# Dilated attention: transposing the probabilities by a product with a diagonal of reciprocal sums

## What is computed

```python
for g, (win, dil) in enumerate(((128, 1), (512, 4), (2048, 16))):
    l = einsum(q * scale, k at q_idx - j * dil) + bias
    p, lse = masked_softmax(l, ok)            # exp(l - m) / sum
    o[g], lses[g] = einsum(p, v), lse
alpha = softmax(stack(lses), axis=0)
o = sum(alpha[..., None] * stack(o))
```

## Time and profile before

| | us |
|---|---|
| median of 3 runs | 1618.79 (1618.61 to 1619.01) |
| the profiled execution | 1611.5 |
| its span | 1609.8 |
| mean granted clock of PE | 0.986 |
| PE busy | 94% of the span |
| DVE, ACT busy | 22%, 22% |

### The profile page before, as it was taken

How to read it: one execution, slowest core, us unless ns; L and a number is a source line. 1 busy time by engine, 2 the same in 40 slices (tenths; PEclk the granted TensorE clock), 3 DMA queues, 4 the chain that set the end, 5 groups by cost and what they waited for, 6 DMA issues and landing times.

```text
span 1609.8 us, 24769 instructions
## 1 busy us (share of the span) xinstructions
PE 1520.3 (94%) x9164; PEld 1186.2 (74%) x9164; DVE 361.7 (22%) x1112; ACT 347.9 (22%) x932; POOL 158.8 (10%) x268
## 2 busy tenths in 40 slices
PE   8998999989899999999988989999889999999996
PEld 5656577767677987777975657777657789777786
DVE  1332234433011211100113242444220122110002
ACT  1132422234111211000123252222331112110003
POOL 2132420000000100000202424000000010000000
PEclk9999999999899999999999999999999999999999
DMA  9686568444355375565847454853716635655543
GB/s 265 155 194 156 150 216 279 151 159 144 126 187 182 106 257 186 187 232 187 244 127 178 121 153 123 291 180 122 239 56 205 215 105 173 243 192 183 196 162 132
DMA packets 212271, 288.06 MB, mean 179 GB/s; under 512 B 13781, under 2 KB 201383, under 8 KB 210888
## 3 DMA queue, kind: packets, MB, share of 16 engines
q1 hardware_dynamic: 194262, 189.01, 38.7%
q10 hardware_dynamic: 7858, 72.49, 12.0%
q0 software_dynamic: 10048, 25.19, 5.8%
HBM read 276.74 MB, written 72.49 MB: 217 GB/s over the span
## 4 chain that ended last, share of the span: by engine, by line
PE 82%; DMA 7%; issue 3%; DVE 2%; ACT 1%; POOLq 1%; SPq 1%; POOL 0%; ACTq 0%; DVEq 0%
PE psum L1469 77%; PE psum L1473 5%; DMA pages<-in_cache_nsa_kv 3%; DMA kv_ring<-in_cache_dil_w 1%; DMA w_ring<-in_w_in 1%; POOLq L702 1%; DMA w_ring<-in_w_ff 1%; ACT regrouped L838 1%; DMA arena<-in_x_sample 0%; DVE pt L1348 0%; SPq L506 0%; SPq L511 0%; DMA kv_ring<-in_cache_nsa_win 0%; SPq L471 0%; ACT xT L1052 0%
## 5 line engine op out<-in xcount | busy, mean ns | idle before, releaser
L1469 PE MATMUL psum<-arena,w_ring 128*128 128x144 f32 (+4 forms) x3584 | 684.1, 353 | 10.1 <-DVE arena L1404 4.8
L1469 PEld LDWEIGHTS psum<-arena,w_ring 128*128 128x128 f32 x3584 | 578.3, 190 | 110.5 <-DVE arena L1404 5.2
L1469 PE MATMUL psum<-xT,w_ring 128*128 128x288 f32 (+1 forms) x1472 | 358.4, 400 | 4.6 <-DMA w_ring<-in_w_in 4.6
L1469 PEld LDWEIGHTS psum<-xT,w_ring 128*128 128x128 f32 x1472 | 269.5, 191 | 80.1 <-issue 9.7
L779 POOL TENSOR_TENSOR arena<-arena 128x144 f32<-128x144 f32 x24 | 11.7, 487 | 653.6 <-DVE arena L1409 653.6
L1444 DVE TENSOR_TENSOR arena<-arena 128x288 f32 x64 | 29.3, 458 | 199.9 <-ACT arena L1062 199.9
L1062 ACT ACTIVATE arena<-psum 128x288 f32<-128x288 f32 x64 | 26.3, 410 | 197.3 <-PE psum L1469 197.3
L1195 DVE COPY arena<-psum 128x512 f32<-128x512 f32 x66 | 45.6, 692 | 78.4 <-PE psum L1473 78.2
L1469 PE MATMUL psum<-arena 64*128 64x128 f32 (+6 forms) x276 | 59.3, 342 | 0.0
L1447 DVE SCALAR_TENSOR_TENSOR arena<-arena,psum 128x288 f32<-128x288 f32 (+1 forms) x20 | 7.0, 390 | 223.0 <-PE psum L1469 223.0
L1473 PE MATMUL psum<-ident,regrouped 128*128 128x128 f32 (+1 forms) x300 | 48.3, 282 | 8.6 <-ACT regrouped L838 7.6
(11 more groups left out here) (206 smaller groups left out, 1214.7 us busy)
## 6 DMA issues: line engine op xcount, KB each, us to landing
w_ring<-in_w_ff SPq DMA_DIRECT2D x64, 1024.0 KB, 5.3
w_ring<-in_w_in SPq DMA_DIRECT2D x44, 1024.0 KB, 7.8
out<-in_cache_dil_w ACTq DMA_DIRECT2D x8, 1984.0 KB
pages<-in_cache_nsa_kv POOLq DMA_DIRECT2D x64, 192.0 KB, 4.5
pages<-in_cache_nsa_kv SPq DMA_DIRECT2D x64, 192.0 KB, 4.5
kv_ring<-in_cache_dil_w SPq DMA_DIRECT2D x20, 512.0 KB, 5.0
w_ring<-in_w_o SPq DMA_DIRECT2D x8, 1024.0 KB, 6.2
out<-in_cache_nsa_win ACTq DMA_DIRECT2D x8, 992.0 KB
```

The source lines that it names most:

```text
L1469: return T.matmul(out, w, x, start=start, stop=stop, **kw)
```

## The change

In dilated steps and in the sample rows' tail, DVE no longer multiplies the exponentials by the reciprocal sums. It multiplies the 128x128 identity by them, which gives a diagonal matrix `diag` (two halves, kept in `kcT`). PE then takes each block of exponentials as weights and the diagonal as the moving operand of an ordinary product, which gives the transposed and scaled block at once. The sparse steps (n < 16) stay as they were.

```diff
+        diag = kcT[:, 0:256].rearrange("p (x n) -> p x n", x=2)
@@ p_scale, n >= 16
-                        v = logit[:, L:L + 768].rearrange("p (g n) -> p g n", g=3)[:, :, 0:nk]
-                        V.tensor_scalar(v, v, S[:, 6:7], None, ALU.mult).then_inc(prob.sem, 1)
+                        V.tensor_scalar(diag[:, par], ident[:, :], S[:, 6:7], None, ALU.mult).then_inc(prob.sem, 1)
@@ the sample rows' tail, DVE
-                V.tensor_scalar(dlogit, dlogit, S[:, 14:15], None, ALU.mult).then_inc(dd_prob.sem, 1)
+                V.tensor_scalar(diag[:, 0], ident[:, :], S[:, 14:15], None, ALU.mult).then_inc(dd_prob.sem, 1)
@@ p_transpose, PE
-                            last = tr(bank(6 + k // 4, 128 * (k % 4), 128), logit[:, L + 256 * i + 128 * m:L + 256 * i + 128 * m + 128])
+                            out, p = bank(6 + k // 4, 128 * (k % 4), 128), logit[:, L + 256 * i + 128 * m:L + 256 * i + 128 * m + 128]
+                            last = tr(out, p) if n < 16 else mm(out, p, diag[:, par])
@@ the sample rows' tail, PE
-                    tr(bank(k // 4, 128 * (k % 4), 128), dlogit[:, 128 * k:128 * k + 128])
+                    mm(bank(k // 4, 128 * (k % 4), 128), dlogit[:, 128 * k:128 * k + 128], diag[:, 0])
                 for k in range(7, 10):
-                    last = tr(bank(k // 4, 128 * (k % 4), 128, 0, ND), dlogit[:, 896 + 32 * (k - 7):928 + 32 * (k - 7)])
+                    last = mm(bank(k // 4, 128 * (k % 4), 128, 0, ND), dlogit[:, 896 + 32 * (k - 7):928 + 32 * (k - 7)], diag[:, 0])
```

## The result

The changed kernel takes 1.0044 of the kernel before, 95% interval 1.0032 to 1.0056: slower by 7.1 us (5.2 to 9.1) of some 1619. Forecast were 8.7 us more, in a range of 3.6 to 12.8.

A forecast was written before the change was run, and what follows sets the result against it. PE was taken to bound the kernel. Per layer 4 x 0.70 + 2 x 0.38 + 1.13 - 0.34 = 4.35 us, two layers 8.70, added to 1618.8: 1627.5 us, range 1622.4 to 1631.6.

The forecast's parts named there:

- What bounds the stretch: Steps 16 to 23 and tail: PE's executed work sets the time; DVE's scaling is hidden in seven of eight steps.
- the 0.34 us: Step 23: DVE's shorter scaling cuts PE's wait from 1.87 to 1.53 us, once per layer.
- The count of passes: The 36 + 10 transpositions per layer on PE become products, one pass each becoming two.
- The rivals of one pass and of four passes: New products on PE: one pass, 1618.1 us (chance 0.04), or four per call, 1646.3 us (chance 0.01).
- The price: Added PE time per block, 0.108 us a pass: even step +0.38, odd step +0.70, tail +1.13 us.
- What is swallowed: Steps 16 and 18: existing DMA waits absorb the added 0.38 us each, so both are priced at nothing.
- The clock: PE around steps 16 and 23 and tail: low-clock losses stay in the sum; one fall more costs some 1.4 us.
- a rival that gives back 4.3 us: Around steps 16 and 23: denser PE work keeps the clock from falling, giving 1623.2 us; chance 0.16.
- DVE's rival: Steps 16 to 23 and tail: each transposition follows DVE's scaling, so 2.6 us per layer return, 1613.6 us; chance 0.03.

The follow-up runs named there:

- DVE's half alone: Kernel before, with DVE scaling the identity and PE still transposing, so the dilated branch is left without its division; against the kernel before: 1.0001 (0.9984 to 1.0018).
- PE's half alone: Kernel before, with the 36 + 10 transpositions per layer made products with the identity, DVE scaling as before; against the kernel before: 1.0056, +9 us.
- the doubled products: Changed kernel with each new product issued twice into the same place: 1.0192 of the kernel before, 24 us above the changed kernel.

## Why the prediction was right, and where its size was off

**What bounds the stretch: right.** DVE's half alone changed nothing that could be measured (1.0001), PE's half alone cost what the whole did, within the intervals (1.0056 and 1.0044). Only step 23 waited for DVE's scaling, and its wait shrank by the 0.34 us that were forecast.

**The count of passes: right.** 144 records for 72 calls, and blocks at two passes a call. The rivals of one pass and of four passes both fall with the rows of the changed kernel, and the doubled products gave 0.11 us a pass again.

**The price: right but for the tail.** An even block was put at 0.93 and took 0.94, an odd one at 1.58 and took 1.60, the tail at 2.44 and took 2.57. The row of six passes with 128-wide weights was the right one to start from. The tail's ten transpositions take 1.28 at full clock, not 1.31. With the measured blocks the sum per layer is 4 x 0.72 + 2 x 0.39 + 1.29 - 0.34 = 4.61, and 9.2 us in all instead of 8.7. The tail's last 0.08 us over that of its passes (1.60 + 8 x 0.111 = 2.49) may be the change to three narrow blocks; that was not tried apart.

**What is swallowed: right in layer 0, not everywhere in layer 1.** Step 16's wait in layer 1 did not shrink (2.32 against 2.29), because the transfer landed later. It took 6.36 us, against 6.34 before, but began 0.74 us behind the stretch's first round and not 0.38; ahead of it a step of SP's queue took 2.94 us and not 2.60. The same wait was 2.02 us in the second profile of the changed kernel and, in layer 0, 2.66 in the second one of the kernel before: where that transfer lands moves by more than the step added.

**The clock: the term that was mis-sized.** The sum took the falls of the clock as they were, and kept their end as a rival that gives back 4.3 us. In the profiled run both falls around step 23 were gone: 9.2 - 1.35 - 1.36 = 6.5 us, and the stretches measured 6.7. That agreement is in part luck, since the second pair of profiles differs by 11.3 us. Two estimates say what the clock gave back over many executions. By the count, half of the falls around step 23 go (9 in 10 became 4 in 10), which is some 0.5 x 2.7 = 1.35 us. By the mean granted clock it is more: it was 0.9839 over the 20 runs of the changed kernel and 0.9806 over 71 runs of the kernel before that were measured apart from them, and among those 71 a run with 0.001 more clock was 1.0 us shorter (a straight line fitted to them), so some 3 us. They leave 9.2 - 1.35 = 7.9 and about 6 us, and both lie in the measured 5.2 to 9.1. Which of the two is right, and which falls besides those of step 23 would have gone, is not settled. By either, the forecast's 8.7 came near because two misses went opposite ways: it left out what the clock gave back, and it had the blocks too cheap by 0.26 us a layer, 0.16 of it in the tail.

The reason that the rival gave first, shorter waits, is not the cause: with the shorter wait and transpositions the clock fell in both layers, and the mean clock did not rise. With products in their place it did (0.9832 against 0.9805, at the old wait of 1.87 us). So the new blocks are what raised it. Whether that is the kind of instruction or only the longer block (1.60 against 0.88 us) was not told apart: no run has a longer block of transpositions at step 23. "TensorE: Matmul & The Clock Gate" of the Trainium skill, PE-mode transpose, says that a transposition does not count as busy for the clock gate in the way that a product does; this is the page that the prediction's rival on the clock means. The counts agree with that (9 of 10 layers with transpositions, 4 of 10 with products), without proving it. The same sentence of that page says that the full clock does not engage for transpose mode, and read by itself this does not fit: the transpositions of the earlier trace rows ran at the full pace, 0.11 us each.

**DVE's rival: rejected as forecast.** PE waited for the scaling in one place per layer, step 23, and what came back there was the 0.34 us; the rival's 2.6 us a layer did not (1.0001 for DVE's half alone).

## What to carry to other kernels

Before work is moved onto the engine that ends last, count in the trace what it executes per call: a float32 product was two passes here, a transposition one, and the engine relieved was waited for in one step of eight. The same count read backwards found the better edit, products with the identity that could be transpositions. What an engine saves is not yet time saved: of the 9.6 us that PE was spared there, 5.7 arrived, because it came sooner to a transfer that it then waited for. Where the rows show the clock falling behind short waits, products that nobody reads can hold it up, and cost nothing if they end before the wait does.

## What the runs showed of the hardware

A block of products with 15-wide weights between transpositions and products with 128-wide ones cost 0.40 us more than the same block as a transposition, where its second pass accounts for 0.11. The weights are 15 wide in both, so their shape alone is not what costs it.

A low clock can also last through work without a gap. In the run with the products twice it was low for some 13 us at step 16 of layer 1, behind the waits that end step 15, while PE was busy all the time (columns as in the earlier trace rows):

```profile
1160.00:1162.00 2.00, 2.00 (x8) 1.59 (x8) 0.00 (x0) 0.00 (x0) 0.00 (x0) 0.50 0.98 330
...
1164.00:1166.00 2.00, 2.00 (x16) 1.65 (x19) 1.44 (x3) 0.94 (x3) 0.00 (x0) 0.50 0.00 0
```

What it did there was rounds of transpositions with their short products, the doubled products of step 16 and its scores. Why the clock stayed low is open.
